# Experts of a mixture layer: the up product as three float32r products of split operands

## The reference

```
h = rmsnorm(x) * (1 + scale2) + shift2
y = (silu(h @ w1[e]) * (h @ w3[e])) @ w2[e]     # w1, w3: 1024 x 512, w2: 512 x 1024
out[token] += weight * y
```

## Time and profile before

| | |
|---|---|
| median of 3 runs | 3943.83 us (3941.31 to 3950.84) |
| the profiled execution | 3946.53 us |
| its span, first to last instruction | 3944.6 us |
| TensorE busy in the span | 3257.8 us (83%) |
| VectorE, ScalarE, GpSimd busy | 1719.3, 865.6, 411.7 us |
| mean granted clock of TensorE | 0.911 |

### The profile page before, as it was taken

How to read it: one execution, slowest core, us unless ns; L and a number is a source line. 1 busy time by engine, 2 the same in 40 slices (tenths; PEclk the granted TensorE clock), 3 DMA queues, 4 the chain that set the end, 5 groups by cost and what they waited for, 6 DMA issues and landing times. The chain is left out here.

```text
span 3944.6 us, 36824 instructions
## 1 busy us (share of the span) xinstructions
PE 3257.8 (83%) x11290; PEld 1726.5 (44%) x11291; DVE 1719.3 (44%) x2657; ACT 865.6 (22%) x1252; POOL 411.7 (10%) x430
## 2 busy tenths in 40 slices
PE   7699999789999999867834999099999999999940
PEld 1366666444444444434412555044444444444410
DVE  0255555547777777569954443411111111111125
ACT  0223232113333333332211222001001001010113
POOL 0000000000000000056600000401111000010114
PEclk9899999869999999979856999599999999999975
DMA  9112121211111111110033332344556744567237
GB/s 338 48 41 62 43 61 43 59 38 33 33 32 29 32 32 27 38 45 0 0 120 104 123 109 106 136 159 173 195 207 230 291 169 164 205 218 262 103 135 276
DMA packets 234516, 445.23 MB, mean 113 GB/s; under 512 B 21511, under 2 KB 94387, under 8 KB 232667
## 3 DMA queue, kind: packets, MB, share of 16 engines
q1 hardware_dynamic: 217853, 397.12, 30.3%
q0 software_dynamic: 16448, 47.31, 3.3%
q10 hardware_dynamic: 160, 0.10, 0.0%
HBM read 366.45 MB, written 86.42 MB: 115 GB/s over the span
## 5 line engine op out<-in xcount | busy, mean ns | idle before, releaser
L1799 PE MATMUL ps_w<-w,block_T 128*128 x1664 | 727.5, 595 | 23.5 <-DVE block_T L1876 19.6
L1799 PEld LDWEIGHTS ps_w<-w,block_T 128*128 128x128 f32 x1664 | 313.7, 190 | 418.1 <-issue 417.7
L764 DVE TENSOR_REDUCE part_max<-ps_max 128x1 f32<-128x512 f32 (+1 forms) x528 | 337.8, 677 | 196.2 <-PE ps_max L660 196.2
L1818 PE MATMUL ps_y<-w,expert_hT 128*128 x832 | 367.5, 594 | 24.9 <-ACT expert_hT L1852 24.9
L741 ACT ACTIVATE probs<-ps_scores 128x1024 f32<-128x1024 f32 x260 | 266.5, 1025 | 488.6 <-PE ps_scores L683 406.8
L1880 DVE TENSOR_TENSOR expert_h<-silu_w,ps_w 128x512 f32<-128x512 f32 x52 | 35.7, 687 | 751.8 <-ACT silu_w L1848 751.8
L380 PE MATMUL ps_proj<-w_in,n1T 128*128 128x512 f32 (+2 forms) x1152 | 347.6, 459 | 2.7 <-DVE n1T L442 2.7
L693 PE MATMUL ps_attn<-probs,v 128*64 128x512 f32 x1040 | 282.7, 623 | 0.0
L1395 PE MATMUL ps_out<-x_and_B,mix_T 128*128 128x512 f32 x576 | 256.1, 603 | 11.2 <-DVE mix_T L1436 11.2
L380 PEld LDWEIGHTS ps_proj<-w_in,n1T 128*128 128x128 f32 x1152 | 196.6, 191 | 142.1 <-issue 131.1
L660 PE MATMUL ps_max<-kT,q_for_max 128*128 128x512 f32 (+1 forms) x528 | 191.8, 437 | 76.2 <-DVE part_max L764 41.5
(11 more groups left out here) (302 smaller groups left out, 3508.4 us busy)
## 6 DMA issues: line engine op xcount, KB each, us to landing
w<-in_w SPq DMA_DIRECT2D x96, 2048.0 KB, 11.3
w_ada_tiles<-in_w_ada SPq DMA_DIRECT2D x12, 2048.0 KB, 9.0
expert_rows<-scratch_y SPq DMA_DIRECT2D x36, 512.0 KB, 5.1
scratch_qT<-qT_stage SPq DMA_DIRECT2D x18, 512.0 KB, 3.5
q_for_max<-scratch_qT SPq DMA_DIRECT2D x36, 256.0 KB, 5.7
q_rounded_twice<-scratch_qT SPq DMA_DIRECT2D x36, 256.0 KB, 4.4
mix_rows<-scratch_mix SPq DMA_DIRECT2D x18, 512.0 KB, 4.4
scratch_h<-h_rows SPq DMA_DIRECT2D x18, 512.0 KB, 2.6
```

Of the source, the lines that this page charges most:

```text
L764: nc.vector.tensor_reduce(mx[:, p, n // H, n % H:n % H + 1], ps_m[:, n % 2, 0:PART], AX.X, ALU.max).then_inc(m_taken, 1)
L1799: last = nc.tensor.matmul(ps[:, :], xT[:, j, k, :], w[:, bass.ds(buf[0], 1), k * DE:(k + 1) * DE], start=(k == 0), stop=(k == KC - 1))
L1818: last = nc.tensor.matmul(ps_y[:, m * 512:(m + 1) * 512], hT[:, j, c, :], w2[:, bass.ds(buf[0], 1), c * D + m * 512:c * D + (m + 1) * 512] ...
```

## The change

The up product is computed with float32r operands, one pass each, instead of fp32. Both operands are split: the rounded part (`xh`, `wh`: a float32r copy) and the rest (`xl`, `wl`: the value minus its rounded part). A product becomes three, rounded by rounded, rounded by rest, rest by rounded. The down product stays plain fp32.

The weights of a block's expert are split anew for each block, in four pieces of 128 x 2048 (two contraction steps of `w1` and `w3`), eight pieces to a pair. ScalarE rounds a piece (`round_weights`), VectorE takes the rest (`rest_weights`), and TensorE uses it (`up`, 12 matmuls). The split pieces lie in a ring of four slots, so that piece s waits until piece s - 4 has been used. Pieces 0 to 2 of a pair are split at the end of the pair before (as pieces 8 to 10). The rows are split the same way in halves (`round_x`, `rest_x`), and `turn` now transposes four chunks into one PSUM tile which both read. The up weights are released for loading when VectorE has taken the rest of the block's last piece (`up_split`), no longer when TensorE has finished. The whole result is copied by ScalarE in two halves, and the down product goes half by half. ScalarE and VectorE read the buffer number from `block_table`, ScalarE with all three entries per block (`of_block`), and the wait for the weights' landing moves from TensorE's `up` to ScalarE's `round_weights`. The table grows from 68 to 70 blocks, as the pieces look ahead.

```diff
-        sp.dma_start(S[name][:, j, :].rearrange("p (k n) -> p k n", n=n), src).then_inc(done, 16)
+        dst = S["w2"][:, j, :] if name == "w2" else S["w13"][:, j, ("w1", "w3").index(name), :]
+        sp.dma_start(dst.rearrange("p (k n) -> p k n", n=n), src).then_inc(done, 16)
...
+    PIECES, RING, PW = 8, 4, 2048
+    UP_END = (3, 7)
...
+        xh = sb("block_T_rounded", [P, 2, KC, P], F32R)
+        xl = sb("block_T_rest", [P, 2, KC, P], F32R)
+        wh = sb("weights_rounded", [P, RING, PW], F32R)
+        wl = sb("weights_rest", [P, RING, PW], F32R)
+        sg = sb("silu_w1", [P, DE])
+        hb = sb("expert_h", [P, DE])
...
+        ps_x = ctx.enter_context(nc.psum_tensor("ps_blockT", [P, KC // 2, P], F32))
+        ps_u = ctx.enter_context(nc.psum_tensor("ps_up", [P, 2, 2, DE], F32))
...
+        ps_y = ctx.enter_context(nc.psum_tensor("ps_y", [P, 2, 512], F32))
...
+        def table_value(eng, b, k, lo, hi):
+            return eng.value_load(S["block_table"][0:1, k, bass.ds(b, 1)], min_val=lo, max_val=hi)
+        def raw_piece(s, buf):
+            return w13[:, bass.ds(buf, 1), :, (s % 4) * 1024:(s % 4 + 1) * 1024]
+        def split_piece(tile, s):
+            return tile[:, s % RING:s % RING + 1, :].rearrange("p o (a n) -> p o a n", a=2)
...
-                    wait_alone(sp, up_ready, before + 1, S["passed"])
+                    wait_alone(sp, up_split, before + 1, S["passed"])
                     wait_alone(sp, up_in[j], i * 32, S["passed"])
                     load_weights(sp, I, S, e, j, ("w1", "w3"), up_in[j])
-                    wait_alone(sp, y_ready, before + 1, S["passed"])
+                    wait_alone(sp, y_ready, before * 2 + 2, S["passed"])
                     wait_alone(sp, down_in[j], i * 16, S["passed"])
                     load_weights(sp, I, S, e, j, ("w2",), down_in[j])
...
-                wait_alone(gp, turned, b - 1, S["passed"])
+                wait_alone(gp, turned, b * 2 - 2, S["passed"])
...
-                wait_alone(gp, y_act, b + 2, S["passed"])
-                wait_alone(gp, y_dve, b + 2, S["passed"])
+                wait_alone(gp, y_taken, b * 2 + 4, S["passed"])
...
+            def turn(b, j, r, i):
                 pe.wait_ge(xg_in[j], i * 16 + 16)
+                wait(pe, xl_done, b * 2 + r)
+                for k in range(KC // 2):
+                    c0 = (r * KC // 2 + k) * P
+                    last = nc.tensor.transpose(ps_x[:, k, :], xg[:, j, c0:c0 + P], S["ident"][:, :])
                 last.then_inc(turned, 1)
+            def products(out, pairs_of, first, last):
+                count = 0
+                for (a_hi, a_lo), (w_hi, w_lo) in pairs_of:
+                    for a, w in ((a_hi, w_hi), (a_hi, w_lo), (a_lo, w_hi)):
+                        count += 1
+                        done = nc.tensor.matmul(out, a, w, start=first and count == 1, stop=last and count == 3 * len(pairs_of))
+                return done
+            def up(b, j, i, s):
+                kk = s % 4
+                if kk == 0:
+                    pe.wait_ge(xl_done, b * 2 + 2)
+                    pe.wait_ge(h_ready, b + 1)
+                pe.wait_ge(lo_done, i * PIECES + s + 1)
+                hi, lo = split_piece(wh, s), split_piece(wl, s)
+                for w in range(2):
+                    both = [((xh[:, j, 2 * kk + k, :], xl[:, j, 2 * kk + k, :]),
+                             (hi[:, 0, w, k * DE:(k + 1) * DE], lo[:, 0, w, k * DE:(k + 1) * DE])) for k in range(2)]
+                    last = products(ps_u[:, j, w, :], both, kk == 0, kk == 3)
+                last.then_inc(used, 1)
             def turn_h(b, j):
+                pe.wait_ge(h_ready, b + 3)
                 pe.wait_ge(hT_ready, b + 1)
                 for c in range(FC):
+                    last = nc.tensor.transpose(ps_h[:, c, :], hb[:, c * P:(c + 1) * P], S["ident"][:, :])
                 last.then_inc(h_turned, 1)
+            def down(b, j, buf, m):
+                if m == 0:
+                    pe.wait_ge(hT_ready, b + 2)
+                    for j2 in range(2):
+                        pe.wait_ge(down_in[j2], buf[1 + j2] * 16)
+                pe.wait_ge(y_taken, b * 2 + m + 1)
+                for c in range(FC):
+                    last = nc.tensor.matmul(ps_y[:, m, :], hT[:, j, c, :], w2[:, bass.ds(buf[0], 1), c, m * 512:(m + 1) * 512],
+                                            start=(c == 0), stop=(c == FC - 1))
                 last.then_inc(y_ready, 1)
...
+            pe.sem_inc(used, RING)
+            pe.sem_inc(y_ready, 2)
+            pe.sem_inc(h_turned, 1)
+            turn(0, 0, 0, 0)
+            turn(0, 0, 1, 0)
+            turn(1, 1, 0, 0)
             with pe.Fori(0, n) as i:
                 b0, b1 = i * 2, i * 2 + 1
+                up(b0, 0, i, 0)
+                up(b0, 0, i, 1)
+                turn(b1, 1, 1, i)
+                up(b0, 0, i, 2)
+                up(b0, 0, i, 3)
+                up(b1, 1, i, 4)
+                turn(b0 + 2, 0, 0, i + 1)
+                up(b1, 1, i, 5)
+                turn_h(b0, 0)
+                up(b1, 1, i, 6)
+                turn(b0 + 2, 0, 1, i + 1)
+                up(b1, 1, i, 7)
                 buf0, buf1 = buffer_of(b0), buffer_of(b1)
+                down(b0, 0, buf0, 0)
                 turn_h(b1, 1)
+                down(b0, 0, buf0, 1)
+                down(b1, 1, buf1, 0)
+                down(b1, 1, buf1, 1)
+                turn(b1 + 2, 1, 0, i + 1)
...
+            def of_block(b):
+                return [table_value(act, b, k, lo, hi) for k, lo, hi in ((0, 0, 1), (1, 1, NE // 2), (2, 1, NE // 2))]
+            def round_weights(i, s, buf):
+                if s % PIECES in (0, 4):
+                    for j in range(2):
+                        wait_alone(act, up_in[j], buf[1 + j] * 32, S["passed"])
+                wait_alone(act, used, i * PIECES + s + 1, S["passed"])
+                act.activation(split_piece(wh, s), raw_piece(s, buf[0]), ACT.Copy).then_inc(hi_done, 1)
+            def round_x(b, j, r):
+                act.wait_ge(turned, b * 2 + r + 1)
+                act.activation(xh[:, j, r * 4:r * 4 + 4, :], ps_x[:, :, :], ACT.Copy).then_inc(xh_done, 1)
+            def silu(b, j, i, s):
+                act.wait_ge(used, i * PIECES + s + 1 + RING)
+                act.wait_ge(h_ready, b + 2)
+                act.activation(sg[:, :], ps_u[:, j, 0, :], ACT.Silu).then_inc(sg_ready, 1)
             def take_hT(b, j):
+                act.wait_ge(h_turned, b + 2)
                 act.activation(hT[:, j], ps_h[:, :, :], ACT.Copy).then_inc(hT_ready, 1)
+            def take_y(b, j, m):
+                act.wait_ge(y_ready, b * 2 + m + 3)
                 act.wait_ge(yb_free, b + 1)
+                act.activation(yb[:, j, m * 512:(m + 1) * 512], ps_y[:, m, :], ACT.Copy).then_inc(y_taken, 1)
+            act.sem_inc(y_taken, 2)
             act.sem_inc(hT_ready, 1)
+            first = of_block(0)
+            round_x(0, 0, 0)
+            round_x(0, 0, 1)
+            for s in range(3):
+                round_weights(0, s, first)
             with act.Fori(0, n) as i:
                 b0, b1 = i * 2, i * 2 + 1
+                buf0, buf1 = of_block(b0), of_block(b1)
+                round_weights(i, 3, buf0)
+                round_x(b1, 1, 0)
+                round_weights(i, 4, buf1)
+                round_weights(i, 5, buf1)
+                round_x(b1, 1, 1)
+                round_weights(i, 6, buf1)
+                round_weights(i, 7, buf1)
+                silu(b0, 0, i, UP_END[0])
+                after = of_block(b0 + 2)
+                round_x(b0 + 2, 0, 0)
                 take_hT(b0, 0)
+                round_weights(i, 8, after)
+                round_x(b0 + 2, 0, 1)
+                silu(b1, 1, i, UP_END[1])
+                round_weights(i, 9, after)
                 take_hT(b1, 1)
+                take_y(b0, 0, 0)
+                round_weights(i, 10, after)
+                take_y(b0, 0, 1)
+                take_y(b1, 1, 0)
+                take_y(b1, 1, 1)
...
+            def rest_weights(i, s, buf):
+                dve.wait_ge(hi_done, i * PIECES + s + 1)
+                nc.vector.tensor_tensor(split_piece(wl, s), raw_piece(s, buf), split_piece(wh, s).bitcast(F32), ALU.subtract).then_inc(lo_done, 1)
+            def release(i, s, split):
+                wait_alone(dve, lo_done, i * PIECES + s + 1, split)
+            def rest_x(b, j, r):
+                dve.wait_ge(xh_done, b * 2 + r + 1)
+                part = slice(r * 4, r * 4 + 4)
+                nc.vector.tensor_tensor(xl[:, j, part, :], ps_x[:, :, :], xh[:, j, part, :].bitcast(F32), ALU.subtract).then_inc(xl_done, 1)
             def gate(b, j):
                 dve.wait_ge(sg_ready, b + 1)
+                dve.wait_ge(h_turned, b + 1)
+                nc.vector.tensor_tensor(hb[:, :], sg[:, :], ps_u[:, j, 1, :], ALU.mult).then_inc(h_ready, 1)
+            dve.sem_inc(h_ready, 2)
```

(106 more changed lines are left out.)

36 lines of the change are left out of this document (6 added, 30 removed).

## The result

The changed kernel takes 3961.5 us in the median (3960.5 to 3967.5), the kernel before 3944.3 beside it: a ratio of 1.0044, interval 1.003 to 1.0059. It is slower by 0.4%, where the prediction had 3907 us and a range that ended at 3952.

What follows compares the result with a forecast made beforehand. TensorE was taken to bound the experts. 101 us gained in 26 pairs, less 18 for late weights, 2 for the start and 44 for the clock, left 37 us: 3907 us as a median, range 3845 to 3952.

Steps and rivals of the forecast that it cites:

- The up product, the splitting, the reads: Experts: up matmuls 0.234 us apart, pieces rounded in 1.9 and subtracted in 2.29 us, six ScalarE register loads 4.2 us.
- Rival E: Up product: f32r matmuls follow closer, 0.2145 us each, 49 us better, 3858 us; chance 0.05.
- It pauses 3.6 us: TensorE, after pieces 0 and 1 of each pair, waits 3.6 us for the second block's rows; a pair becomes 42.9 us.
- After it I find no wait: Rest of each pair after the pause: no further TensorE wait; nearest is the first block's gate, ready 0.9 us early.
- The clock: Behind each pair's pause: some 3.4 us at half clock lose 1.7 us, 44 us in 26 pairs.
- Rival A: Experts: the clock stays up despite the pauses, 81 us gained, 3863 us; chance 0.17.
- C: Behind the pauses: clock falls last twice as long, 88 us lost instead of 44, 3951 us, no change; chance 0.13.
- Late weights: Three pairs: ScalarE waits for a second block's up weights, TensorE loses 6 us in each, 18 in all.
- Rival D: ScalarE's earlier need meets late weights in many pairs, 6 us each; 3967 us with ten further pairs; chance 0.09.
- Rival B: Loop top: register loads do not hold ScalarE up, no pause or clock fall, about 3780 us; chance 0.08.
- Gathers and scatters ... cost nothing: Each pair: they wait for the same events as before, with some 30 us to land, and cost nothing.

Runs made afterwards that it cites:

- one_table: Changed kernel with one single-column Silu ahead of ScalarE's expert loop, so no table load is left inside it: 3941.8 us, ratio 0.9989 to the kernel before.
- p_table_early: Changed kernel with TensorE's six buffer-number reads moved from behind up piece 7 to between up piece 1 and the turn: 3918.7 us, ratio 0.9941 to the kernel before.
- as_costed: Changed kernel with the edits of one_table and p_table_early together: 3898.8 us, ratio 0.9867 to the kernel before.
- fill16: Changed kernel with sixteen added float32r matmuls between up piece 1 and the turn of every pair: 3925.4 us, ratio 0.9959 to the kernel before.
- few_loads: Changed kernel with ScalarE reading one register instead of six ahead of piece 3: 3892.8 us, ratio 0.9880 to the kernel before.
- rows_first: Changed kernel with the edits of one_table, few_loads and p_table_early, and GpSimd issuing next-pair gathers earlier: 3798.9 us, ratio 0.9629 to the kernel before.

## Why the prediction was wrong

**The up product, the splitting, the reads.** Right. The step of the up matmuls is 0.23 us (0.234 forecast), pieces take 1910 and 2292 ns (1.9 and 2.29), ScalarE's gap for its reads and the branch is 4.20 us (4.6 forecast, 0.4 of it for the branch, which no row shows by itself). Rival E falls with the step: the Trainium skill's 216 ns (TensorE: Matmul & The Clock Gate, section Back-to-back issue gap) is not reached by these matmuls, which start 0.23 us apart.

**"It pauses 3.6 us".** The first failed step. The place and the releaser were right, and so were the parts of the cause that it names; the walk from take_y to piece 3 left out a table load. The prediction counted one per turn, "as before", put it in ScalarE's sum and not on the path. In the kernel before, the first activation of a turn was silu, and its load stood there. The new loop has two, and one stands before the first rounding, where ScalarE is what TensorE waits for. It costs 1.28 us in each of 25 pauses, which are 5.0 us and not 3.6. The Trainium skill (ScalarE activation tables: per-element evaluation and per-set limits, section Table sets in the compiler and the runtime) says that loads are placed block by block; the trace agrees, in that a Copy at the loop's top gets one (26 at L1898) although one_table runs the same Copies with none in the loop.

**"After it I find no wait".** The second failed step. The prediction priced six register reads on ScalarE from TensorE's six in the earlier trace rows, and did not put those same six of TensorE on its path. In the kernel before these ran under a down product, which began at 2705.25 and lasted 7.10 us. In the new order they stand behind up piece 7 with the down product behind them, and cost 1.17 us in every pair, 30 us; p_table_early gained 41, with less work at the lower clock.

**The two together** are 70 us (as_costed), where the prediction missed by 55. The kernel without them has a ratio of 0.9867, which is 3892 us beside 3944: 15 us better than the 3907 of the sum. Not every term of the sum fits, and that it comes so close is in part luck. On one side the pair before is 46.93 us in the mean and not 46.79, 4 us more to gain from, and TensorE's work in a pair is 38.6 us and not 39.3, 18 us in 26 pairs; this is an estimate from 1058 us of busy time less 54 for the lower clock. On the other side those 54 us are 10 more than the 44 of the sum, and gathered rows cost 10 that were put at nothing. Of the other 13, 6 come from the profiled execution, which took that much more than the median; the rest is within the interval of that ratio, 8 us to either side.

**The clock.** Right in place, too small in size: 44 us forecast, some 55 by fill16. The prediction took 3.4 us of work at half the clock for each pause, from the input phase; in the pair shown it is 5.0 us, which at 0.43 instead of 0.23 us a step lose 2.3 and not 1.7. In all, 136 us of TensorE's busy time lie in half-clock stretches in the changed kernel and 116 in as_costed; 0.20 / 0.43 of that, an estimate, is 63 and 54 us. Rival A falls. C, falls twice as long for 88 us, is not reached either; the cost lies between it and the forecast.

**Late weights.** 18 us forecast in three pairs; they are 4.5, 4.3 and 6.5 us above the median, 15. ScalarE stands there for 6.3 to 6.8 us, as forecast, but TensorE waits 8.8 us in all for the late pieces and not 18; the rest lies in the slower matmuls behind. Where the pause is shorter that wait is longer: 15.6 us in as_costed, 25.6 in few_loads, 34.8 in rows_first. The near agreement here is in part luck. Rival D gave almost the measured time, 3961 to 3967, by another way: ScalarE waited for weights 5 times and 23.1 us in all, not in ten further pairs. It was right by chance only.

**Rival B**, that the reads do not hold ScalarE up, falls by few_loads.

**"Gathers and scatters ... cost nothing".** Right for this kernel (1.7 us) and wrong once the pause is shorter: 10.1 us in as_costed, 38.3 in few_loads.

The change does gain what its arithmetic promises, when nothing at the loop's top stands before it: TensorE's work is less, and in rows_first the pairs are 7 us shorter in the median than before. In the changed kernel this was given back in three waits of TensorE (124.8, 30.4 and 8.8 us) and in the clock behind the longest.

## What to carry to other kernels

Walk a loop's turn for each engine through everything in its queue, register reads and table loads included: they cost nothing while they run beside the work of the engine that sets the time, and show as soon as that engine has to wait for them. A stall of TensorE can have two prices, its length and the slower matmuls behind it, as the pauses of 5.0 us had here, so a short stall in every turn can eat a change that removes real work. When a wait goes, look at once for the next chain: here the edits to the queues were worth 129 us, and a gather order that is worth nothing alone gave 35 more.

## What the runs showed of the hardware that had not been expected

Adding 416 matmuls to a loop made it 34 us faster, by the granted clock (0.99 instead of 0.93): the pause with what was put into it did not get shorter. A loop over the same activations ran with two table loads a turn or with none, according to what was run just ahead of it, 1283 ns each. Six register reads in a row held ScalarE's queue and TensorE's queue for about 4 us each: 0.66 us a read on ScalarE and 0.76 on TensorE.
